# Array tiles in pairs and 512-column products in a three-FFN fp32 kernel

## What is computed

```python
def rwkv7_recurrence(r, decay, k, v, kk, a):           # 8 heads of 64, 256 steps
    def step(S, inp):
        sa = jnp.einsum('bhij,bhj->bhi', S, -kk_t)
        S = (S * w_t[:, :, None, :] + sa[..., None] * (kk_t * a_t)[:, :, None, :]
             + v_t[..., None] * k_t[:, :, None, :])
        y_t = jnp.einsum('bhij,bhj->bhi', S, r_t)
...
w = -jax.nn.softplus(-(w0 + jnp.tanh(wl) @ w2)) - 0.5  # wl, al: 64 wide
a = jax.nn.sigmoid(a0 + al @ a2)
...
def stick_breaking_attention(q, k, v):                 # 8 heads of 64, blocks of 128
    z = jnp.einsum('bhqd,bhkd->bhqk', qb, kb) * scale
    ...
    outs.append(jnp.einsum('bhqk,bhkd->bhqd', attn, vb))
...
def conv_ffn(x, g, w_up, conv_w, conv_b, w_down):
    h = rms_norm(x, g) @ w_up
    ...
    return (jax.nn.silu(gate) * val) @ w_down
```

## Time and profile before

| what | value |
|---|---|
| median of 3 runs | 1288.37 us (1287.01 to 1290.18) |
| profiled execution | 1290.41 us, its span 1288.4 us |
| TensorE busy | 1206.2 us, 94% of the span, 9872 matmul instructions |
| VectorE busy | 893.4 us, 69% |
| ScalarE busy | 665.2 us, 52% |
| GpSimd busy | 367.7 us, 29% |
| mean granted TensorE clock | 0.979 |
| read from HBM | 186.52 MB, 146 GB/s |

### The profile page before, as it was taken

The page is one execution under the profiler, slowest core; times in us unless marked ns, Lnnn a source line. Parts: engine busy times, 40 slices in busy tenths (PEclk is TensorE's granted clock), DMA queues, the critical chain, the costliest instruction groups (busy, mean ns, idle before and its releaser), DMA issues.

```text
span 1288.4 us, 25633 instructions
## 1 busy us (share of the span) xinstructions
PE 1206.2 (94%) x9872; PEld 1145.8 (89%) x9872; DVE 893.4 (69%) x1281; ACT 665.2 (52%) x975; POOL 367.7 (29%) x339
## 2 busy tenths in 40 slices
PE   5888898999999999999999799999999979999998
PEld 5877777989999999999988799999998659999998
DVE  5767545443766889875757588887577667888952
ACT  3566663324444555554446665554444664656531
POOL 3323101000001355531200234554127112455500
PEclk9889998999999999999999899999999989999999
DMA  7533220022554655555442255555553315555552
GB/s 254 190 112 134 92 82 1 4 81 83 197 181 166 207 179 179 176 173 181 164 162 99 99 171 181 175 180 176 180 180 132 117 47 166 179 180 179 180 171 75
DMA packets 53702, 188.82 MB, mean 147 GB/s; under 512 B 6000, under 2 KB 6128, under 8 KB 53232
## 3 DMA queue, kind: packets, MB, share of 16 engines
q1 hardware_dynamic: 52016, 182.47, 41.7%
q10 hardware_dynamic: 1600, 5.12, 1.2%
HBM read 186.52 MB, written 1.05 MB: 146 GB/s over the span
## 4 chain that ended last, share of the span: by engine, by line
PE 78%; DVE 10%; ACT 8%; issue 2%; POOL 1%; DMA 0%; POOLq 0%; ACTq 0%; DVEq 0%
PE psA L453 67%; PE psB L453 11%; ACT arena L1064 4%; DVE arena L1633 2%; DVE rounded L1630 2%; ACT L1064 2%; DVE arena L1630 2%; ACT rounded L1064 2%; DVE rounded L1633 1%; DMA arena<-in_par 0%; DVE arena L1936 0%; POOL rounded L1543 0%; POOL arena L1455 0%; PE psB L695 0%; PE psB L666 0%
## 5 line engine op out<-in xcount | busy, mean ns | idle before, releaser
L453 PE MATMUL psA<-rounded,rounded 128*128 128x256 f32 (+1 forms) x7968 | 1025.6, 291 | 55.6 <-DVE rounded L1630 29.3
L453 PEld LDWEIGHTS psA<-rounded,rounded 128*128 128x128 f32 x7968 | 994.9, 194 | 82.8 <-issue 31.4
L1630 DVE TENSOR_TENSOR rounded<-arena,rounded 128x1024 fp32r<-128x1024 f32 (+1 forms) x354 | 445.4, 1278 | 108.8 <-ACT rounded L1064 105.4
L1064 ACT ACTIVATE rounded<-arena 128x1024 fp32r<-128x1024 f32 (+1 forms) x438 | 386.9, 928 | 224.1 <-PE psA L453 109.7
L1455 POOL TENSOR_TENSOR arena<-arena 128x256 f32<-128x256 f32 (+1 forms) x126 | 164.0, 1306 | 656.1 <-ACT arena L1064 259.7
L1064 ACT ACTIVATE arena<-arena 128x256 f32<-128x256 f32 (+6 forms) x288 | 150.4, 555 | 189.6 <-DVE arena L1630 141.3
L1633 DVE SCALAR_TENSOR_TENSOR arena<-arena 128x255 f32<-128x255 f32 (+4 forms) x334 | 174.4, 565 | 45.5 <-ACT arena L1064 35.4
L453 PE MATMUL psB<-arena 64*64 64x64 f32 (+8 forms) x1832 | 185.2, 281 | 7.1 <-ACT arena L1064 3.5
L453 PEld LDWEIGHTS psB<-arena 64*64 64x64 f32 (+4 forms) x1832 | 143.8, 161 | 35.7 <-issue 20.6
L1545 POOL TENSOR_TENSOR rounded<-arena,rounded 128x256 f32 (+1 forms) x66 | 92.0, 1395 | 9.5 <-POOL rounded L1543 8.0
L1064 ACT ACTIVATE arena<-psA 128x512 f32<-128x512 f32 (+1 forms) x52 | 25.5, 496 | 103.2 <-PE psA L453 102.8
(11 more groups left out here) (66 smaller groups left out, 144.9 us busy)
## 6 DMA issues: line engine op xcount, KB each, us to landing
arena<-in_w SPq DMA_DIRECT2D x344, 512.0 KB, 3.2
arena<-in_x SPq DMA_DIRECT2D x2, 512.0 KB, 6.3
arena<-in_mem ACTq DMA_DIRECT2D x2, 512.0 KB, 6.1
arena<-in_x ACTq DMA_DIRECT2D x1, 1024.0 KB, 4.9
arena<-in_con ACTq DMA_DIRECT2D x1, 1024.0 KB, 6.7
out<-arena SPq DMA_DIRECT2D x1, 1024.0 KB, 3.9
arena<-in_con ACTq DMA_DIRECT2D x1, 992.0 KB, 4.8
arena<-in_par ACTq DMA_DIRECT2D x1, 264.0 KB, 3.9
```

Source lines behind the costliest of these rows:

```text
L453: ins_ = nc.tensor.matmul(o, l, r, start=start, stop=stop, skip_group_check=shared)
L1064: return nc.scalar.activation(o, i, f, **kw)
L1630: return V.tensor_tensor(o, a, b, op)
```

## The change

- The down projections (`project_sum`, `mm_sum`): per weight block one product of the upper weight with upper and rest of the input side by side (512 columns, a bank to itself) and one of the rest of the weight with the upper input (256 columns, into the first half). There are eight outputs per FFN in place of four; VectorE adds both halves of a bank to the residual (`residual_sum`).
- dl and al, z and qd: the products of the two row halves (partitions 0 to 63, 64 to 127) are issued in alternation, into two banks. The quads' second pair is one product of 256 columns, and VectorE empties a quad by one operation.
- so, ut, st and y: products whose 64 useful output columns go to partitions 0 to 63 or 64 to 127 of one bank, issued in alternation. ut has one bank per token block in place of two, y two banks in place of four, and the readers copy all 128 partitions at once.
- Buffers of the middle stage move (`QM`, X, XC, mg), and the places for rounded data are merged.

```diff
-SM = (["rx", "rm", "dl0", "dl1", "al0", "al1", "gl0", "gl1", "kn0", "kn1",
+SM = (["rx", "rm", "dl0", "al0", "dl1", "al1", "gl0", "gl1", "kn0", "kn1",
...
-        quad = view(z1, 16, 384)
-        MP = view(z1 + 24, 16, P)
-        X = view(z1 + 24, 2, 512)
-        XC = view(z1 + 28, 2, 512)
+        QM = view(z1, 2, 16 * 256)
+        quadA = QM[:, 0, :].rearrange("p (i n) -> p i n", i=16)
+        quadR = QM[:, 1, :].rearrange("p (i n) -> p i n", i=16)
+        X = view(base, 2, 512)
+        XC = view(z1 + 40.5, 2, 512)
...
+        def both(x, k):
+            a, b = fr(x[0][:, k, :]), fr(x[1][:, k, :])
+            assert a.tensor.name == b.tensor.name
+            return bass.AP(tensor=a.tensor, offset=min(a.offset, b.offset),
+                           ap=[list(a.ap[0]), [abs(a.offset - b.offset), 2]] + [list(y) for y in a.ap[1:]])
...
+                    close(last, name)
+            def mm_sum(o, w, x, k, start, stop):
+                mm(o[:, :], w[0], both(x, k), start, False)
+                return mm(o[:, 0:T], w[1], fr(x[0][:, k, :]), False, stop)
+            def project_sum(names, src, nk=KD, ready_k=None):
+                for n, name in enumerate(names):
+                    o = open_(name)
+                    for k in range(nk):
+                        w = weights(1)
+                        if ready_k and n == 0:
+                            ready_k(k)
+                        last = mm_sum(o, w, src, k, k == 0, k == nk - 1)
...
-            for name, lo, hi, col, ch, need in (("dl", 0, 64, 0, 12, 1), ("al", 64, 128, 0, 12, 1),
-                                               ("gl", 0, 128, 512, 13, 2)):
-                for u in range(2):
-                    o = open_(f"{name}{u}")
-                    ready(pe, "lora_in", need)
-                    for m in range(2):
-                        c = 2 * u + m
-                        last = mm(o[:, m * T:(m + 1) * T], lora[lo:hi, col + c * P:col + (c + 1) * P],
-                                  pb[lo:hi, ch, :], True, True)
-                    close(last, f"{name}{u}")
+            for u in range(2):
+                o = [open_(f"{n}{u}") for n in ("dl", "al")]
+                ready(pe, "lora_in", 1)
+                for m in range(2):
+                    cs = slice((2 * u + m) * P, (2 * u + m + 1) * P)
+                    last = [mm(o[n][:, m * T:(m + 1) * T], lora[64 * n:64 * n + 64, cs],
+                               pb[64 * n:64 * n + 64, 12, :], True, True) for n in range(2)]
+                close(last[0], f"dl{u}")
+                close(last[1], f"al{u}")
...
-                    mm(o[:, hh * T:(hh + 1) * T], sbv[:, 0, c * P:(c + 1) * P], zb[:, 2 * c + hh, 0:T],
-                       True, False)
-                    last = mm(o[:, hh * T + P:(hh + 1) * T], sbv[:, 1, c * P:(c + 1) * P],
+                    mm(o[64 * hh:64 * hh + 64, 0:T], sbv[:, 0, c * P + 64 * hh:c * P + 64 * hh + 64],
+                       zb[:, 2 * c + hh, 0:T], True, False)
+                for hh in range(2):
+                    last = mm(o[64 * hh:64 * hh + 64, P:T], sbv[:, 1, c * P + 64 * hh:c * P + 64 * hh + 64],
...
-            for h in range(8):
-                sb_scores(h)
+            for c in range(4):
+                sb_scores(c)
...
-            for i in range(16):
-                t, h = i // 8, i % 8
-                c, b = h // 2, 64 * (h % 2)
-                o = open_(f"qd{i}")
+            for i in range(0, 16, 2):
+                t, c = i // 8, i % 8 // 2
+                o = [open_(f"qd{i}"), open_(f"qd{i + 1}")]
...
-                mm(o[:, 0:T], K1[b:b + 64, c, ts], ARv[b:b + 64, :, c, ts], True, True)
-                for m in (0, 1):
-                    last = mm(o[:, (2 + m) * P:(3 + m) * P], LC[b:b + 64, c, ts],
-                              ARv[b:b + 64, 1 - m, c, ts], True, True)
-                close(last, f"qd{i}")
+                for n, b in enumerate((0, 64)):
+                    mm(o[n][:, 0:T], K1[b:b + 64, c, ts], ARv[b:b + 64, :, c, ts], True, True)
+                for n, b in enumerate((0, 64)):
+                    close(mm(o[n][:, T:2 * T], LC[b:b + 64, c, ts], ARv[b:b + 64, :, c, ts], True, True),
+                          f"qd{i + n}")
...
-                for cp in range(2):
-                    o = open_(f"ut{t}.{cp}")
-                    pe.wait_ge(*freed(f"l5t{t}"))
-                    pe.wait_ge(*freed(f"tr{t}.a"))
-                    for j in range(4):
-                        last = mm(o[:, j * P:(j + 1) * P],
-                                  tok[:, t * 4 + 3, (2 * cp + j // 2) * P:(2 * cp + j // 2 + 1) * P],
-                                  XTt(t * 8 + 4 * cp + j), True, True)
-                    close(last, f"ut{t}.{cp}")
+                o = open_(f"ut{t}")
+                pe.wait_ge(*freed(f"l5t{t}"))
+                pe.wait_ge(*freed(f"tr{t}.a"))
+                for h in range(8):
+                    b = 64 * (h % 2)
+                    last = mm(o[b:b + 64, h // 2 * P:(h // 2 + 1) * P], tok[:, t * 4 + 3, h * 64:(h + 1) * 64],
+                              XTt(t * 8 + h), True, True)
+                close(last, f"ut{t}")
...
-                        s = slice(c * P, (c + 1) * P)
-                        mm(o[:, s], tok[hs, t * 4 + 1, s], SA[hs, t, s], True, False)
-                        last = mm(o[:, s], tok[hs, t * 4 + 2, s], tok[hs, t * 4, s], False, True)
+                        for n, src in ((1, SA[:, t, :]), (2, tok[:, t * 4, :])):
+                            for b in (0, 64):
+                                s = slice(c * P + b, c * P + b + 64)
+                                last = mm(o[b:b + 64, c * 64:(c + 1) * 64], tok[hs, t * 4 + n, s], src[hs, s],
+                                          n == 1, n == 2)
...
-                o = open_(f"y{c}")
-                cs = slice(c * P, (c + 1) * P)
-                for hh in range(2):
-                    for t in range(TT):
-                        i = t * 8 + 2 * c + hh
-                        s = slice(hh * T + t * P, hh * T + (t + 1) * P)
-                        mm(o[:, s], SA[:, t, cs], quad[:, i, P:T], True, False)
-                        mm(o[:, s], tok[:, t * 4, cs], quad[:, i, 2 * P:3 * P], False, False)
-                        for q in range(max(2 * t, 1), 2 * t + 2):
-                            last = mm(o[:, hh * T + q * CH:hh * T + (q + 1) * CH], ST[q][:, c, :],
+                o = open_(f"y{c // 2}") if c % 2 == 0 else o
+                for t in range(TT):
+                    to = c % 2 * T + t * P
+                    for n, src in ((0, SA[:, t, :]), (1, tok[:, t * 4, :])):
+                        for b in (0, 64):
+                            last = mm(o[b:b + 64, to:to + P], src[:, c * P + b:c * P + b + 64],
+                                      quadR[:, t * 8 + 2 * c + b // 64, n * P:(n + 1) * P], n == 0, False)
+                    for q in range(max(2 * t, 1), 2 * t + 2):
+                        for b in (0, 64):
+                            last = mm(o[b:b + 64, to + q % 2 * CH:to + q % 2 * CH + CH], ST[q][:, c, b:b + 64],
...
-                close(last, f"y{c}")
+                if c % 2:
+                    close(last, f"y{c // 2}")
...
-                for u in range(KD // 2):
-                    name = f"down{f}.{u}"
-                    o = open_(name)
-                    for m in range(2):
-                        for k in range(KF):
-                            w = weights(1)
-                            if u == 0 and m == 0:
-                                ready(pe, "act_ready", f * UPS + k + 1)
-                            last = mm3(o[:, m * T:(m + 1) * T], w, part((AH, AL), slice(0, P), k),
-                                       k == 0, k == KF - 1)
-                    close(last, name)
+                project_sum([f"down{f}.{m}" for m in range(KD)], (AH, AL), KF,
+                            lambda k: ready(pe, "act_ready", f * UPS + k + 1))
...
-                o = take(f"so{c}")
-                A(ys[0:64, 4 + c, :], o[0:64, 0:T], ACT.Copy).then_inc(sem("act_aux"), 1)
-                release(A(ys[64:128, 4 + c, :], o[64:128, T:2 * T], ACT.Copy), f"so{c}")
+                release(A(ys[:, 4 + c, :], take(f"so{c}")[:, 0:T], ACT.Copy), f"so{c}")
...
+            def by_pair(ap):
+                return ap.rearrange("p (n m k) -> p n m k", n=2, m=2)
...
-                o = take(f"qd{i}")
-                mark(tt(quad[:, i, :], o[:, 0:384], cst("mask4")[:, 0:384], ALU.mult))
-                settle()
-                release(tt(MP[:, i, :], o[:, 384:512], cst("mask4")[:, 384:512], ALU.mult), f"qd{i}")
+                release(tt(QM[:, :, i * T:(i + 1) * T].rearrange("p m (n k) -> p n m k", n=2),
+                           by_pair(take(f"qd{i}")[:, :]), by_pair(cst("mask4")), ALU.mult), f"qd{i}")
...
+            def residual_sum(names, s, tag=None, g=None):
+                for k, name in enumerate(names):
+                    o = take(name)
```

(9 more changed lines are left out.)

93 lines of the change are left out of this document (47 added, 46 removed).

## The result

The changed kernel takes 1272.3 us (median of five runs: 1272.0, 1272.1, 1272.3, 1278.3, 1278.3) against 1288.4, so 16.1 us less between the medians. The ratio of the two sets of runs, in which the two at 1278 count as well, is 0.9895, with a 95% interval of 0.9877 to 0.9913: 1.1% faster. The forecast was 1267.0 in a range of 1259 to 1278. The time lies in the range, 5.3 us above the forecast.

A forecast was written before the change was run, and what follows sets the result against it. The prediction took TensorE as the bound, with 78% of the span in the chain of waits. Its terms summed to 21.5 us, taking the profiled 1290.4 to 1268.9 and the median to 1267, in a range of 1259 to 1278.

The forecast's parts named there:

- The y products: Products for y on TensorE: issued as pairs on half arrays they take 5.0 us against 12.5, saving 7.5 us.
- Rival 1: Column pairs in U, state, y and stick-breaking values do not overlap: 10.8 us saved, 1277.6 us; chance 0.15.
- U and state: U and state products on TensorE: issued as half-array pairs, they save 1.8 us for U and 2.6 us for state.
- ten changes of shape: Stick-breaking, U and y products become column-tiled: ten tile-shape changes at 0.1 us each, a loss of 1.0 us.
- Quads: The 16 quad units: VectorE empties each by one operation, not two, 0.65 us a unit; saves 2.2 us.
- so: Stick-breaking values: four groups of 1.3 us become 0.65, the first two ahead of ScalarE's table load; saves 1.4 us.
- dl and al: Decay and rate projections: pairing removes one slot of two products, at a granted clock of 0.65; saves 1.1 us.
- The down stage: FFN down projections: a block takes 227 + 120 = 347 ns against 360; saves 6.1 us in three FFNs.
- The bounds (360 and 324): Down projections, ns a block: 360 saves 0 (chance 0.08, 1273.0 us); 324 saves 16.6 us (chance 0.05, 1256.4 us).
- The feed: Weight supply in the down projections: VectorE's 2.0 us a slot stays hidden, as a slot of 8 blocks lasts 2.78 us.
- the allowance from the profiled run to the median: Whole kernel: the median of the runs lies 2.0 us below the profiled execution, so 1268.9 becomes 1266.9 us.
- low-clock stretches that move: Low-clock stretches move because idle times move; one costs or returns 2 to 4 us, near 1270 or 1263; chance 0.07.

The follow-up runs named there:

- unpaired: The changed kernel with its half-array products of U, state and y ordered so that neighbours lie on the same tile; 1278.4 us, ratio 0.9929.
- late_rests: The changed kernel with one wait more: GpSimd's eight subtractions for the lower memory rows start only after VectorE's decay chain; 1271.0 us, ratio 0.9866.

## Why the prediction was right, and where it was off

- **The y products.** 7.5 us forecast, 12.5 down to 5.04 measured from start to start. This mechanism was right, and its bound too: without overlap y would have taken 10 us. Rival 1 is out. The page "TensorE: Matmul & The Clock Gate" of the Trainium skill, Part 3, says that a weight load overlaps products only where the row group differs. The new pairs share their row group and each product has a load of 64 columns of its own, and two of them together still cost 110 ns (one alone takes 109 in unpaired). The trace does not agree with the page here; that nothing at all would overlap was the forecast's own step from it. The same page of the Trainium skill, Back-to-back issue gap, gives 2.5 ns over the columns for a product in isolation. In the stream here the mixed block is 33 ns over the 320 of its columns, 17 for each product.
- **U and state.** 1.8 and 2.6 forecast; 2.3 for the U stretch, 3 x 0.87 = 2.6 for state. The separate -1.0 for ten changes of shape shows in neither U nor y, whose measured gains have six of these changes inside.
- **Quads.** 2.2 forecast. VectorE's operations give 2.5, of which 1.9 reach the first U product (46.7 to 44.8 us from the first quad).
- **so.** The table load comes 1.6 us sooner against the first so product, where 1.7 were forecast; the sum took 1.4. These small edits were read from the traces and not tried one by one.
- **dl and al.** 1.1 forecast. 9.3 us became 6.7 up to the product behind, but before has 6.8 us of it at 1.2 GHz and after 3.4, half of the difference being 1.7: 0.9 is left for the pairing.
- **The middle stage as a whole.** Its terms (all but the down ones) sum to 15.6, and the lead at its end was 19.5. Up to there before has 34 us at 1.2 GHz and after 24, which can explain all of the 3.9; the terms as measured above sum to 16.8, which leaves 2.7 to the clock.
- **The down stage is the term that was mis-sized.** "227 + 120 = 347 ns against 360" took each price from a steady stream of one length. Alternating, a block cost 353.3: three stages gave 3.1 us and not 6.1. The bounds (360 and 324) held it. That is 3.0 us less than forecast.
- **The term that was missing.** The feed was worked out for the down stage only ("2.0 us a slot, hidden"), and rightly: inside the down stages of the changed kernel no step is longer than 241 ns. The up loops, whose code had not changed, have no term at all. There VectorE hands over its slots late, and 0.8 and 2.5 us went. With the down stage that is 6.3 us less than forecast in the profiled execution; the middle stage's 3.9 more and the later clock stretches (-2.4, +1.5) leave 18.2 of 21.5. The other 2.0 of the 5.3 are the allowance from the profiled run to the median: before's profiled run lay 2.0 over its median, the changed kernel's lies on it. The full-clock times say the same more shortly: 15.1 us gained (from 1260.4 to 1245.3), and the forecast less its two misses is 21.5 - 3.0 - 3.3 = 15.2. The middle stage was thus well forecast. Part of the closeness of the profiled run is luck, though: there the clock, which has no term in the sum, gave back up to 3.0 of the 6.3 us (3.9 - 2.4 + 1.5).
- **The low clock.** The case "low-clock stretches that move" got 0.07 and should have had far more. The stretches move from kernel to kernel (only late_rests has those of the changed kernel, to 0.4 us). The same pieces of work, first after, then before, with the same gap and the same busy time of TensorE (9.48 us):

```profile
300.00:312.00 12.00, 9.48 (x69) 9.28 (x68) 9.80 (x13) 5.33 (x7) 0.00 (x0) 0.88 0.46 137
```

```profile
319.50:331.50 12.00, 9.48 (x79) 9.28 (x78) 9.75 (x13) 5.33 (x7) 0.00 (x0) 1.00 0.45 139
```

One is at 0.88 and gets 69 products through, the other at 1.00 and 79. Nothing of the change lies there.

## What to carry to other kernels

Products on half an array pay when neighbours in the queue lie on different tiles, by rows or by columns. For 128 moving columns the order is the whole gain here; for 64 the half array alone gave 58 ns an instruction instead of 112, and the order the rest. Price a mixed stream as a mixed stream: the steady price of each part was 2% too low for the alternation here, half of the hoped gain. And when a change shifts the time at which a tight loop is entered, look at the loop, even if none of its lines changed: where VectorE and GpSimd share the work, their meeting is a cost of its own, and taking one small operation off GpSimd was worth more than the whole down edit (4.2 us against 2.2 on the kernel before). Last, when edits do not add up, look at the clock of every run before you doubt the edits.
